# Earlier weight slabs, halved refills and unrolled pairs in the experts of a transformer block, one Trainium2 core

## The chip, the core and the metric

The kernel is one program on one core of a Trainium2 chip. It computes two transformer blocks for a sequence of 512 tokens, model width 1024, in float32. The metric is the device time of one execution in microseconds (us). Three runs of the kernel before gave 3689.02, 3692.55 and 3693.8 us; their median, 3692.55 us, is the time before.

## The reference, cut to what matters

The change touches the end of the mixer and the expert layer of the first block. Everything else (the mixer's branches, all of the second block) is left as it is.

```python
N_EXPERTS, EXPERT_FF, EC_CAPACITY = 16, 1024, 2        # D_MODEL 1024, SEQ 512

def ec_moe(h, router, w1, w3, w2):
    b_, n, _ = h.shape
    cap = EC_CAPACITY * n // N_EXPERTS                 # 64 tokens an expert
    aff = jax.nn.softmax(jnp.einsum('bld,de->ble', h, router).astype(F32), axis=-1)
    gate, idx = lax.top_k(jnp.swapaxes(aff, 1, 2), cap)
    bidx = jnp.arange(b_)[:, None, None]
    xe = h[bidx, idx]
    hid = jax.nn.silu(jnp.einsum('becd,edf->becf', xe, w1)) * jnp.einsum('becd,edf->becf', xe, w3)
    ye = jnp.einsum('becf,efd->becd', hid, w2) * gate[..., None].astype(h.dtype)
    return jnp.zeros_like(h).at[bidx, idx].add(ye)

# in first_block
x = x + g1 * rms_norm(ml, norm1_post[l])
h2 = rms_norm(x, norm2_pre[l]) * (1 + sc2) + sh2
x = x + g2 * rms_norm(ec_moe(h2, router[l], exp_w1[l], exp_w3[l], exp_w2[l]), norm2_post[l])
```

Each expert chooses its 64 tokens. The weights of the 16 experts are 16 x 3 x 4 MB = 201 MB, all of which must come from HBM.

## The kernel before, in words

The program is a chain of stages. A stage (function `stage`) is one block with a part for each engine; the parts meet only through semaphores, and between stages all engines meet at a barrier. Within a stage each engine runs its instructions in the order written. All large loads are issued by SyncE (SP), so their order is the order of SP's part.

Three stages lie around the change.

**settle** (the first of its three calls) multiplies the mixer's merged output `m` by `w_out`, adds it to `x`, normalises, stores `x` (L1760) and the normalised rows `xn_dram` (L1763) tile by tile, and computes the router's logits. SP first issues its loads (L1747 to L1757, the last one `se_hw`, the router's weights), then the stores of the four token tiles as VectorE finishes them. The normalised tile of a token tile t has one of two places in `se_xn`; for t = 2 and 3 VectorE waits until the store of tile t - 2 has landed (above L1924).

**choice_experts** routes and runs the experts. VectorE finds the 64 largest affinities of each expert in eight rounds (L2124 to L2127), and writes the token numbers to `chosen` (L2134). Then it builds `scat`, the matrices that will add the results back (L2137, eight instructions), and GpSimd gathers the 128 rows of the first pair of experts from `xn_dram` into `ex_xg` (L2043, an indirect DMA). TensorE transposes them (L2051, `turn`), VectorE scales them into `ex_xs` (L2144, `take_tokens`), and the products begin.

The experts are taken in eight pairs. The weights are cut into 96 slabs of 2 MB (128 partitions of 16 KB), in the order of use, 12 to a pair: eight for the products with w1 and w3 (`up`), four for w2 (`down`). One product (`both_experts`, L2060) takes two slabs, one for each expert of the pair, in 16 matmuls for each slab. After four products the hidden rows are transposed (L2072) and copied to `ex_hidT` (L2109), the next pair's rows are transposed (L2051), and the two down products follow; their results go to `ye` (L2161). The pairs are a loop on each engine (`Fori`), the last one outside it on TensorE and VectorE.

The slabs lie in `ex_ring`, six places, with a semaphore `slab_in` and a semaphore `slab_free` each. SP fills six places when the stage begins (L2024), and each further slab when both halves of its place's old slab have been used to the end (L2028):

```python
sp.wait_ge(slab_free[n % RING], i * 2 + (n // RING + 1))
sp.dma_start(ring[:, n % RING, :, :], w_slabs[bass.ds(i * PER + n, 1)].rearrange("a p k n -> p (a k) n")
             ).then_inc(slab_in[n % RING], 16)
```

**settle** (the second call) multiplies `scat` by `ye`, adds the result to `x` and goes on to the second block.

Of the kernel before, what the change touches and what calls it, by code (L numbers as in the profile page):

```python
# [20 lines left out]
P = 128  # L21
D = 1024
# [32 lines left out]
@contextmanager  # L55
def stage(nc):

    with ExitStack() as stack:
        s = Sems(nc, stack)
        with nc.Block() as block:  # L60
            yield s, block, stack
        nc.clear_and_free_semaphores(list(s.all.values()))
        nc.all_engine_barrier()  # L63
# [1649 lines left out]
def settle(nc, cst, source, rows, norm, x_in, x_out, cols, head, lg, xT=None, xn_dram=None, xn_keep=None):  # L1713
# [9 lines left out]
    with ExitStack() as keep:  # L1723
# [17 lines left out]
        with stage(nc) as (s, block, _):  # L1741
# [3 lines left out]
            def _(sp):  # L1745
# [240 lines left out]
CAP = 2 * SEQ // NE  # L1986


def choice_experts(nc, cst, lg, positions, idx, scat, xn_dram, a_col, sh_col, ring, w_slabs, ye):

    RING, PER = 6, 12
    NTT, PAIRS_E, ROUNDS = SEQ // P, NE // 2, CAP // 8
    ident, CT = cst("ident"), 6
    with ExitStack() as keep:
# [3 lines left out]
        affT = sb("ct_affT", [NE, 2, SEQ])  # L2001
# [7 lines left out]
        hidT = sb("ex_hidT", [P, KC, P])  # L2009
        ps = keep.enter_context(nc.psum_tensor("ex_ps", [P, 8, 512], F32, allow_name_mangling=True))  # L2010
        with stage(nc) as (s, block, _):
            slab_in = [s.named(f"slab_in{n}") for n in range(RING)]
            slab_free = [s.named(f"slab_free{n}") for n in range(RING)]
            halves = [slice(64 * j, 64 * j + 64) for j in range(2)]
            up = lambda h, m: 4 * h + 2 * m
            down = lambda h: 8 + 2 * h
            used = lambda i, n: i * 2 + (n // RING + 2)

            @block.sync
            def _(sp):  # L2020

                sp.dma_start(every[:, :], positions.broadcast_to([P, SEQ])).then_inc(s.every_in, 16)
                for n in range(RING):
                    sp.dma_start(ring[:, n, :, :], w_slabs[n]).then_inc(slab_in[n], 16)  # L2024

                def load(i, n):
                    sp.wait_ge(slab_free[n % RING], i * 2 + (n // RING + 1))
                    sp.dma_start(ring[:, n % RING, :, :], w_slabs[bass.ds(i * PER + n, 1)].rearrange("a p k n -> p (a k) n")  # L2028
                                 ).then_inc(slab_in[n % RING], 16)

                for n in range(RING, PER):
                    load(0, n)
                with sp.Fori(1, NE // 2) as i:
                    for n in range(PER):
                        load(i, n)

            @block.gpsimd
            def _(pool):
                pool.wait_ge(s.placed, 1)
                for g in range(NE // 2):  # L2040
# [5 lines left out]
            def _(pe):  # L2046
                def turn(i):

# [5 lines left out]
                def both_experts(i, n, src, bank):  # L2054

                    for j in range(2):
                        pe.wait_ge(slab_in[(n + j) % RING], i * 32 + 16 * ((n + j) // RING + 1))
                    for k in range(KC):
                        for j in range(2):
                            mm = pe.matmul(ps[halves[j], bank, :], src[:, k, halves[j]], ring[:, (n + j) % RING, k, :], start=k == 0, stop=k == KC - 1)  # L2060
                            if k == KC - 1:
                                mm.then_inc(slab_free[(n + j) % RING], 1)

                def pair(i, last):
                    pe.wait_ge(s.xs_ready, i + 1)
                    for h in range(2):
                        pe.wait_ge(s.hid_ready, i * 2 + (h + 1))
                        for m in range(2):
                            both_experts(i, up(h, m), xs, 2 * h + m)
                    pe.wait_ge(s.hid_ready, i * 2 + 4)  # L2070
                    for k in range(KC):
                        mm = pe.transpose(ps[:, 4 + k // 4, P * (k % 4):P * (k % 4) + P], hid[:, P * k:P * k + P], cst("ident"))  # L2072
                    mm.then_inc(s.hid_turned, 1)
                    pe.wait_ge(s.hidT_ready, i * 2 + 2)
                    if not last:
                        turn(i + 1)
                    for h in range(2):
                        pe.wait_ge(s.ye_kept, i * 2 + (h + 1))
                        both_experts(i, down(h), hidT, 6 + h)
# [9 lines left out]
                for n in range(RING):  # L2089
                    pe.sem_inc(slab_free[n], 1)  # L2090
                pe.sem_inc(s.hid_turned, 1)
                turn(0)
                with pe.Fori(0, NE // 2 - 1) as i:
                    pair(i, False)
                pair(NE // 2 - 1, True)

            @block.scalar
            def _(act):
                act.wait_ge(s.shifted, 1)
                act.activation(aff[:, :, :], aff[:, :, :], ACT.Exp).then_inc(s.exped, 1)  # L2100
                with act.Fori(0, NE // 2) as i:
                    act.wait_ge(s.hid_turned, i + 1)
                    for h in range(2):
                        n = up(h, 0) + 1
                        act.wait_ge(slab_free[n % RING], used(i, n))
                        act.activation(hid[:, 512 * h:512 * h + 512], ps[:, 2 * h, :], ACT.Silu).then_inc(s.silu, 1)  # L2106
                    act.wait_ge(s.hid_turned, i + 2)
# [4 lines left out]
            def _(dve):  # L2112
# [25 lines left out]
                dve.sem_inc(s.hid_ready, 2)  # L2138
                dve.sem_inc(s.ye_kept, 2)
# [8 lines left out]
                def pair(i, last):  # L2148
                    for h in range(2):
                        n = up(h, 1) + 1  # L2150
                        dve.wait_ge(s.silu, i * 2 + (h + 1))
                        dve.wait_ge(slab_free[n % RING], used(i, n))
                        part = hid[:, 512 * h:512 * h + 512]
                        dve.tensor_tensor(part, part, ps[:, 2 * h + 1, :], ALU.mult).then_inc(s.hid_ready, 1)  # L2154
                    if not last:
                        take_tokens(i + 1)
                    for h in range(2):
                        n = down(h) + 1
                        dve.wait_ge(slab_free[n % RING], used(i, n))
                        out = ye[:, bass.ds(i, 1), 512 * h:512 * h + 512].rearrange("p a n -> p (a n)")  # L2160
                        dve.tensor_copy(out, ps[:, 6 + h, :]).then_inc(s.ye_kept, 1)  # L2161

                take_tokens(0)
                with dve.Fori(0, NE // 2 - 1) as i:
                    pair(i, False)
                pair(NE // 2 - 1, True)


# [1059 lines left out]
def program(nc, a, out):  # L3228

    with ExitStack() as keep:  # L3230
# [14 lines left out]
        wide = lambda n: logits[:, 0:4 * n].rearrange("p (t n) -> p t n", t=4)  # L3245
        with ExitStack() as mixer:
# [14 lines left out]
            with ExitStack() as mg:  # L3261
# [63 lines left out]
```

## Time and profile before

| | |
|---|---|
| median of three runs | 3692.55 us |
| the profiled execution | 3690.78 us, its span 3689.0 us |
| TensorE busy | 3200.2 us, 87% of the span |
| VectorE, ScalarE, GpSimd busy | 40%, 27%, 1% |
| DMA over the whole span | mean 150 GB/s |
| DMA from about 2029 to 2398 us (4 of the 40 slices) | 428 GB/s in each |
| first settle stage | about 1889 to 1976 us |
| choice and experts | about 1976 to 2486 us |
| idle of TensorE before L2060, waiting for `ex_ring` | 63.1 us (of 66.1) in the up products, 10.9 us (of 12.9) in the down products |

The span is the time between the first and the last recorded instruction; the execution's own time is 1.8 us longer. Numbers of instructions on TensorE are counted twice, as matmuls (PE) and as weight loads (PEld), which run beside each other. A busy share says how much of a stretch an engine worked, not whether the next engine waited for it. For that the views of waits and of order in time are read.

### The profile page before, as it was taken

The page shows a single profiled execution, that of the slowest core. Times are in us where ns is not written, and L with a number is a line of the kernel's source. Part 1 is how long each engine was busy: PE and PEld are TensorE (multiplying, and loading weights), DVE is VectorE, ACT ScalarE, POOL GpSimd, SP SyncE. Part 2 cuts the span into 40 slices and gives each one's busy share as a digit, 9 for nine tenths or more (in the row PEclk, how much of TensorE's full clock was granted, in tenths as well). Part 3 has the DMA queues.
Part 4 walks back from the last instruction along what each step waited for, and adds up shares of the span by engine and source line. Part 5 has one row for each costly group of instructions (what it writes and reads, how often), then busy time and mean ns, then how long its engine had stood idle before and what let it go on. Part 6 is the DMA issues. An engine that isn't in the chain of part 4 may idle for free. (4 is left out here: it accounts for less than half of the span.)

```text
span 3689.0 us, 54736 instructions
## 1 busy us (share of the span) xinstructions
PE 3200.2 (87%) x23420; PEld 1783.0 (48%) x23420; DVE 1488.1 (40%) x3058; ACT 998.2 (27%) x1963; POOL 45.7 (1%) x65
## 2 busy tenths in 40 slices
PE   7889998889889999889995878777999999984996
PEld 3566666666765555544442323224454555541332
DVE  3666667666645676520014101003333324332122
ACT  2343443433213645620011000002233242320001
POOL 0000000000000000000000000000000000000000
PEclk9999999999879999889997999998999999986998
DMA  4112221122231222252024999982311111027998
GB/s 173 55 60 63 64 81 61 58 64 63 63 104 52 85 73 78 86 173 74 40 104 182 428 428 428 428 367 111 117 49 72 46 71 46 1 105 301 413 417 335
DMA packets 107203, 555.11 MB, mean 150 GB/s; under 512 B 30960, under 2 KB 33760, under 8 KB 82272
## 3 DMA queue, kind: packets, MB, share of 16 engines
q1 hardware_dynamic: 100832, 532.94, 37.4%
q0 software_dynamic: 3456, 12.58, 0.9%
q10 hardware_dynamic: 2688, 6.29, 0.4%
q8 instruction: 175, 2.87, 0.3%
q14 instruction: 52, 0.43, 0.0%
HBM read 518.03 MB, written 33.74 MB: 150 GB/s over the span
## 5 line engine op out<-in xcount | busy, mean ns | idle before, releaser
L2337 PE MATMUL mh_ps<-mh_w_ahead,xmT 128*128 128x512 f32 x768 | 336.3, 592 | 0.0
L2060 PE MATMUL ex_ps<-ex_ring,ex_xs 128*64 128x512 f32 x1024 | 243.7, 632 | 66.1 <-DMA ex_ring<-expert_slabs_in 63.1
L493 PE MATMUL rw_ps<-hT,rw_w 128*128 128x512 f32 (+1 forms) x640 | 258.9, 535 | 6.1 <-PEq L63 5.8
L2337 PEld LDWEIGHTS mh_ps<-mh_w_ahead,xmT 128*128 128x128 f32 x768 | 144.6, 190 | 167.0 <-issue 165.0
L2060 PEld LDWEIGHTS ex_ps<-ex_ring,ex_xs 128*64 128x64 f32 x1024 | 87.6, 145 | 221.7 <-issue 221.7
L1258 PE MATMUL sg_ps<-hTp,sg_w 128*128 128x512 f32 x384 | 170.3, 596 | 0.0
L493 PEld LDWEIGHTS rw_ps<-hT,rw_w 128*128 128x128 f32 x640 | 113.1, 192 | 89.6 <-issue 79.8
L2321 PE MATMUL mh_ps<-xmT,mh_w_ahead 128*128 128x512 f32 x256 | 127.0, 631 | 14.6 <-PEq L63 8.4
L2154 DVE TENSOR_TENSOR ex_hid<-ex_hid,ex_ps 128x512 f32<-128x512 f32 x16 | 11.0, 687 | 296.2 <-PE ex_ps L2060 296.2
L2060 PE MATMUL ex_ps<-ex_ring,ex_hidT 128*64 128x512 f32 x512 | 116.9, 610 | 12.9 <-DMA ex_ring<-expert_slabs_in 10.9
L1780 PE MATMUL se_ps<-se_w,se_mT 128*128 128x512 f32 x256 | 113.5, 600 | 7.6 <-DMA se_w<-w_out_in 7.6
L2964 PE MATMUL ge_ps<-ge_ring,ge_xs 128*64 128x512 f32 x512 | 116.1, 607 | 2.7 <-DVE ge_xsq L3059 2.7
L1258 PEld LDWEIGHTS sg_ps<-hTp,sg_w 128*128 128x128 f32 x384 | 73.8, 193 | 90.9 <-issue 90.8
L1482 DVE SCALAR_TENSOR_TENSOR sg_acc<-sg_ps,sg_par,sg_acc 128x510 f32<-128x510 f32 (+3 forms) x176 | 110.5, 628 | 6.2
L1297 PE MATMUL sg_ps<-sg_wz,hTp 128*128 128x512 f32 x256 | 112.2, 592 | 0.0
L1673 PE MATMUL mg_ps<-mg_pb,ybT 128*128 128x512 f32 x256 | 111.0, 592 | 0.0
L2106 ACT ACTIVATE ex_hid<-ex_ps 128x512 f32<-128x512 f32 x16 | 9.6, 597 | 361.5 <-PE ex_ps L2060 361.5
L1326 PEld LDWEIGHTS sg_ps<-sg_xdt,sg_kern 128*128 128x128 f32 x512 | 73.0, 211 | 46.3 <-issue 26.3
L1326 PE MATMUL sg_ps<-sg_xdt,sg_kern 128*128 128x64 f32 x512 | 72.9, 291 | 19.6 <-DVE sg_yacc L1545 10.4
L916 DVE TENSOR_TENSOR rw_xb<-rw_xb,rw_e 128x31 f32<-128x31 f32 (+15 forms) x248 | 85.2, 343 | 8.5
L1378 ACT ACTIVATE sg_kern<-sg_kern,tok 128x128 f32<-128x128 f32 x256 | 81.1, 390 | 26.5 <-DMA sg_kern<-cum_dram 26.5
L915 DVE TENSOR_TENSOR rw_e<-rw_low,rw_xb 128x31 f32<-128x31 f32 (+15 forms) x248 | 84.5, 341 | 6.9
(594 smaller groups left out, 5231.6 us busy)
## 6 DMA issues: line engine op xcount, KB each, us to landing
ex_ring<-expert_slabs_in SPq DMA_DIRECT2D x96, 2048.0 KB, 18.3
ge_ring<-expert_slabs_in SPq DMA_DIRECT2D x52, 2048.0 KB, 12.5
mh_w_ahead<-head_slabs_in SPq DMA_DIRECT2D x16, 2048.0 KB, 7.8
rw_mod_w<-mod_w_in SPq DMA_DIRECT2D x64, 384.0 KB, 4.1
rw_mod_w<-ada_in SPq DMA_DIRECT2D x64, 256.0 KB, 3.3
sg_kern<-cum_dram SPq DMA_DIRECT2D x64, 256.0 KB, 3.2
rw_w<-rw_slabs_in SPq DMA_DIRECT2D x8, 1536.0 KB, 7.0
sg_w<-xbc_blocks_in SPq DMA_DIRECT2D x24, 512.0 KB, 5.0
```

The costliest lines, as they stand in the source:

```text
L493: mm = pe.matmul(where[j, part], w[:, k, P * j:P * j + P], tokens, start=k == 0, stop=k == KC - 1)
L916: link(dve.tensor_tensor(xb[:, m:32, 0:m], xb[:, m:32, 0:m], part, ALU.subtract))
L1258: mm = pe.matmul(ps[:, A[j % 2], :], w[:, j, k, :], hTp[:, k, :], start=k == 0, stop=k == KC - 1)
L1297: mm = pe.matmul(ps[:, A[c % 2], :], hTp[:, k, P * c:P * c + P], wz[:, k, :], start=k == 0, stop=k == KC - 1)
L1326: mm = pe.matmul(ps[:, IN, v], kern[:, m % RING, P * h:P * h + P], xdt[:, m // 2 % 3, v], start=n % 4 == 0 and h == 0, stop=n % 4 == 3 and ...
L1482: link(dve.scalar_tensor_tensor(out[:, lo:hi], src[:, lo + i - 2:hi + i - 2], tap(i), out[:, lo:hi], ALU.mult, ALU.add))
L1673: mm = pe.matmul(ps[:, 4 * (n % 2) + j, :], src[:, k, off + P * t:off + P * t + P], w[:, k, :], start=k == 0, stop=k == nk - 1)
L1780: mm = pe.matmul(ps[:, ybank(t, h), :], left[:, k, tile(t)], right(k, h), start=k == 0, stop=k == KB - 1)
L2060: mm = pe.matmul(ps[halves[j], bank, :], src[:, k, halves[j]], ring[:, (n + j) % RING, k, :], start=k == 0, stop=k == KC - 1)
L2321: mm = pe.matmul(ps[:, 5 + b % 2, :], w[:, 0, k, P * b:P * b + P], xmT[:, k, :], start=k == 0, stop=k == KC - 1)
L2337: mm = pe.matmul(ps[:, 4 + t, :], xmT[:, k, P * t:P * t + P], w[:, slot, k, :], start=k == 0, stop=k == KC - 1)
L2964: mm = pe.matmul(ps[both[b], U[n], :], xs[:, i % 2, k, both[b]], up(2 * n + b)[:, k, :], start=k == 0, stop=k == KC - 1)
```

## The change

It has six parts.

1. Four slabs are loaded during the first settle stage, behind its own loads and ahead of its stores: slab 0 into a place of its own (`ex_first`), and slabs 8, 9 and 10 into `ye` and `scat`, which are not written until later.
2. The ring has eight places instead of six. With the three in `ye` and `scat`, which are used once, eleven slabs can lie in place. The choice stage begins with slabs 1 to 4; slabs 5 to 7 wait until the first gather has landed (`s.x_in`).
3. From slab 11 on a slab comes in two halves of 1 MB (four of the eight blocks k, 8 KB in each partition), each issued when the product that uses the place's old slab has got past that half. One semaphore `used`, raised twice by each product, replaces the `slab_free` semaphores.
4. The loops over the pairs are unrolled on all engines.
5. `scat` is built in the second pair, after `take_tokens`, instead of ahead of the first product.
6. `m` is allocated at the other end of the SBUF and freed after settle, `xmT` is allocated after the experts, and `affT` lies in `ex_hid`.

```diff
# settle, SyncE
                 sp.dma_start(hw[:, :, :], head_w).then_inc(s.head_in, 16)
+                for dst, src, landed in ahead:
+                    sp.dma_start(dst, src).then_inc(landed, 16)
                 for t in range(NTT):
# choice_experts
+EX_RING = 8
-    RING, PER = 6, 12
+    PER, REG, SPARE = 12, len(ring), len(spare)
+    FIRST = REG + SPARE
+            before = lambda g: g - REG if g >= FIRST + REG else g - FIRST
+            part_used = lambda g, part: 2 * (g // 2) + part + 1
# SyncE
                 sp.dma_start(every[:, :], positions.broadcast_to([P, SEQ])).then_inc(s.every_in, 16)
-                for n in range(RING):
-                    sp.dma_start(ring[:, n, :, :], w_slabs[n]).then_inc(slab_in[n], 16)
...
-                for n in range(RING, PER):
-                    load(0, n)
-                with sp.Fori(1, NE // 2) as i:
-                    for n in range(PER):
-                        load(i, n)
+                for g in range(1, 5):
+                    sp.dma_start(ring[g], w_slabs[g]).then_inc(slab_in[g], 16)
+                sp.wait_ge(s.x_in, 16)
+                for g in range(5, REG):
+                    sp.dma_start(ring[g], w_slabs[g]).then_inc(slab_in[g], 16)
+                for g in range(FIRST, TOTAL):
+                    dst, landed, _ = home(g)
+                    for half in range(2):
+                        ks = slice(4 * half, 4 * half + 4)
+                        sp.wait_ge(s.used, part_used(before(g), half))
+                        sp.dma_start(dst[:, ks, :], w_slabs[g][:, ks, :]).then_inc(landed, 16)
# TensorE
-                            if k == KC - 1:
-                                mm.then_inc(slab_free[(n + j) % RING], 1)
+                        if k % 4 == 3:
+                            mm.then_inc(s.used, 1)
...
-                with pe.Fori(0, NE // 2 - 1) as i:
-                    pair(i, False)
-                pair(NE // 2 - 1, True)
+                for i in range(PAIRS_E):
+                    pe.wait_ge(s.xs_ready, i + 1)
...
# VectorE
-                dve.wait_ge(s.every_in, 16)
-                for g in range(PAIRS_E):
-                    dve.tensor_scalar(scat[:, g, :], every[:, :], place[:, 0, g:g + 1], place[:, 1, g:g + 1], ALU.is_equal, ALU.mult)
...
                     if i + 1 < PAIRS_E:
                         take_tokens(i + 1)
+                    if i == 1:
+                        dve.wait_ge(s.every_in, 16)
+                        dve.wait_ge(s.used, down_used(0, 1))
+                        for g in range(PAIRS_E):
+                            dve.tensor_scalar(scat[:, g, :], every[:, :], place[:, 0, g:g + 1], place[:, 1, g:g + 1], ALU.is_equal, ALU.mult)
# program
+            spare = [as_slab(ye[:, 0:4, :]), as_slab(ye[:, 4:8, :]), scat[:, :, :]]
+                       ahead=[(first[:, :, :], a["expert_slabs"][0], early.named("slab_in0"))] +
+                             [(spare[n], a["expert_slabs"][EX_RING + n], early.named(f"spare_in{n}")) for n in range(len(spare))])
```

How the rows of three places stand, read from the built programs (no times in them). The first is SP in the first settle stage; before:

```order
L1753 DMA se_w<-w_out_in 128x4096
L1754 DMA se_g<-norm_pre_in 128x8
L1755 DMA se_sc<-mod 128x8x1
L1756 DMA col_sh<-mod 128x8x1
L1757 DMA se_hw<-router_in 128x128
L1760 DMA x<-se_x 128x1024
L1763 DMA xn_dram<-se_xn 128x1024
```

and now (the stores' lines have moved by two in the text):

```order
L1755 DMA se_sc<-mod 128x8x1
L1756 DMA col_sh<-mod 128x8x1
L1757 DMA se_hw<-router_in 128x128
L1759 DMA ex_first<-expert_slabs_in 128x4096
L1759 DMA ye<-expert_slabs_in 128x4096 x2
L1759 DMA scat<-expert_slabs_in 128x4096
L1762 DMA x<-se_x 128x1024
L1765 DMA xn_dram<-se_xn 128x1024
```

Four loads of 2 MB (4096 floats in each partition) stand between the router's weights and the first store.

The second is SP at the start of the choice stage. Before, with the first instructions of its loop:

```order
L2022 DMA ct_every<-positions_in 128x512
L2024 DMA ex_ring<-expert_slabs_in 128x4096 x6
L2028 DMA ex_ring<-expert_slabs_in 128x4096 x6
L2033 UNCONDITIONAL_BRANCH
L2033 ISA
L2028 ISA
L2028 DMA ex_ring<-expert_slabs_in 128x4096
```

and now:

```order
L2032 DMA ct_every<-positions_in 128x512
L2034 DMA ex_ring<-expert_slabs_in 128x4096 x4
L2037 DMA ex_ring<-expert_slabs_in 128x4096 x3
L2043 DMA ex_first<-expert_slabs_in 128x2048 x2
L2043 DMA ex_ring<-expert_slabs_in 128x2048 x14
L2043 DMA ex_first<-expert_slabs_in 128x2048 x2
```

Four slabs stand where six did, three more follow them, and all later loads are halves (2048 floats), 170 of them.

The third is VectorE from the choice of the tokens on. Before:

```order
L2134 CAST chosen<-ct_place 128x8
L2137 TENSOR_SCALAR scat<-ct_every,ct_place 128x512 x8
L2144 TENSOR_SCALAR ex_xs<-ex_ps,col_a,col_sh 128x128 x8
L2164 UNCONDITIONAL_BRANCH
L2164 ISA
L2152 REGISTER_ALU
L2154 TENSOR_TENSOR ex_hid<-ex_hid,ex_ps 128x512
```

and now:

```order
L2136 CAST chosen<-ct_place 128x8
L2141 TENSOR_SCALAR ex_xs<-ex_ps,col_a,col_sh 128x128 x8
L2151 TENSOR_TENSOR ex_hid<-ex_hid,ex_ps 128x512 x2
L2141 TENSOR_SCALAR ex_xs<-ex_ps,col_a,col_sh 128x128 x8
L2161 COPY ye<-ex_ps 128x512 x2
L2151 TENSOR_TENSOR ex_hid<-ex_hid,ex_ps 128x512 x2
L2141 TENSOR_SCALAR ex_xs<-ex_ps,col_a,col_sh 128x128 x8
L2158 TENSOR_SCALAR scat<-ct_every,ct_place 128x512 x8
L2161 COPY ye<-ex_ps 128x512 x2
```

The eight instructions that build `scat` have moved from ahead of the first pair to the middle of the second.

## Rows read from the trace of the kernel before

**Rows 1.** The profile page, costliest groups, the products of the experts:

```profile
L2060 PE MATMUL ex_ps<-ex_ring,ex_xs 128*64 128x512 f32 x1024 | 243.7, 632 | 66.1 <-DMA ex_ring<-expert_slabs_in 63.1
L2060 PE MATMUL ex_ps<-ex_ring,ex_hidT 128*64 128x512 f32 x512 | 116.9, 610 | 12.9 <-DMA ex_ring<-expert_slabs_in 10.9
```

**Rows 2.** Stretches: length, busy times (count), then granted clock, DMA share, GB/s:

```profile
1911.00:1932.00 21.00, 21.00 (x50) 9.31 (x49) 7.96 (x21) 6.81 (x18) 0.00 (x0) 1.00 0.14 54
1998.00:2009.00 11.00, 0.39 (x2) 0.28 (x2) 4.27 (x12) 1.28 (x1) 1.20 (x1) 0.50 1.00 424
2017.00:2025.00 8.00, 8.00 (x32) 2.71 (x30) 0.00 (x0) 0.00 (x0) 0.00 (x0) 0.75 0.00 1
2060.00:2460.00 400.00, 316.03 (x1380) 118.74 (x1378) 33.79 (x74) 22.50 (x32) 4.68 (x5) 0.95 1.01 428
```

**Rows 3.** TensorE in order of time, the first pair of experts and the last:

```profile
2011.05 1.97 PE L2051 MATMUL ex_ps<-consts,ex_xg 128*128 128x128 f32 x8 [12.49 <-DMA ex_xg<-xn_dram,chosen]
2016.04 30.10 PE L2060 MATMUL ex_ps<-ex_ring,ex_xs 128*64 128x512 f32 x128 [3.02 <-DVE ex_xs L2144]
2049.28 1.09 PE L2051 MATMUL ex_ps<-consts,ex_xg 128*128 128x128 f32 x8 [1.24 <-ACT ex_hidT L2109]
2050.29 7.09 PE L2060 MATMUL ex_ps<-ex_ring,ex_hidT 128*64 128x512 f32 x32
2109.24 1.59 PE L2051 MATMUL ex_ps<-consts,ex_xg 128*128 128x128 f32 x8 [1.24 <-ACT ex_hidT L2109]
...
2458.36 8.50 PE L2060 MATMUL ex_ps<-ex_ring,ex_xs 128*64 128x512 f32 x32 [2.70 <-DMA ex_ring<-expert_slabs_in]
2477.91 7.09 PE L2060 MATMUL ex_ps<-ex_ring,ex_hidT 128*64 128x512 f32 x32 [0.83 <-DVE ye L2161]
2486.66 34.57 PE L1780 MATMUL se_ps<-ye,scat 128*128 128x512 f32 x80 [1.66 <-PEq L63]
```

**Rows 4.** SP in order of time, 1970 to 2520 us (start, length, line, count):

```profile
1976.52 3.34 SPq L2024 DMA_DIRECT2D ex_ring<-expert_slabs_in  x6
2025.55 431.11 SPq L2028 DMA_DIRECT2D ex_ring<-expert_slabs_in  x90
```

**Rows 5.** GpSimd in order of time, the gathers of the first two pairs:

```profile
1999.47 1.20 POOL L2043 DMA_INDIRECT ex_xg<-xn_dram,chosen  x1 [965.96 <-DVE chosen L2134]
2013.29 0.94 POOL L2043 DMA_INDIRECT ex_xg<-xn_dram,chosen  x1 [12.63 <-PE ex_ps L2051]
```

**Rows 6.** The tile ex_xg, its gathers' time to landing, over the whole span:

```profile
DMA to landing us min/median/max: 4.3/10.8/11.5
```

**Rows 7.** VectorE in order of time, settle's third tile and the building of scat:

```profile
1948.60 0.76 DVE L1924 TENSOR_SCALAR se_xn<-se_x,se_rx 128x1024 f32<-128x1024 f32 x1
1999.09 3.73 DVE L2137 TENSOR_SCALAR scat<-ct_every,ct_place 128x512 f32<-128x512 f32 x8
```

**Rows 8.** DMA queues from 2060 to 2460 us (q0 is GpSimd's, q1 SP's):

```profile
q1 hardware_dynamic: 11568, 168.56, 99.0%
q0 software_dynamic: 743, 2.65, 1.6%
q8 instruction: 1, 0.02, 0.0%
```

**Rows 9.** SP in order of time in the first settle stage:

```profile
1908.36 2.84 SPq L1757 DMA_DIRECT2D se_hw<-router_in  x1
1928.40 0.32 SPq L1763 DMA_DIRECT2D xn_dram<-se_xn  x1
```

**Rows 10.** The page: the count of instructions, and the queue that fetches them:

```profile
span 3689.0 us, 54736 instructions
...
q8 instruction: 175, 2.87, 0.3%
```

**Rows 11.** DMA queues from 3370 to 3680 us, the second block's experts:

```profile
q1 hardware_dynamic: 8547, 106.58, 83.4%
q0 software_dynamic: 1152, 4.19, 3.8%
```

More of the change, by code:

```diff
@@ L55, in stage @@
 @contextmanager
-def stage(nc):
+def stage(nc, carried={}):
     with ExitStack() as stack:
@@ L1710, in _, with settle @@
                     dve.tensor_tensor(m[:, t, cols], ga_n, gb_n, ALU.add).then_inc(s.merged, 1)
-def settle(nc, cst, source, rows, norm, x_in, x_out, cols, head, lg, xT=None, xn_dram=None, xn_keep=None):
+def settle(nc, cst, source, rows, norm, x_in, x_out, cols, head, lg, xT=None, xn_dram=None, xn_keep=None, ahead=()):
     NTT, H, KB = SEQ // P, 2, 8
@@ L1986, with choice_experts @@
 CAP = 2 * SEQ // NE
-def choice_experts(nc, cst, lg, positions, idx, scat, xn_dram, a_col, sh_col, ring, w_slabs, ye):
-    RING, PER = 6, 12
+EX_RING = 8
+def choice_experts(nc, cst, lg, positions, idx, scat, xn_dram, a_col, sh_col, ring, spare, early, w_slabs, ye):
+    PER, REG, SPARE = 12, len(ring), len(spare)
+    FIRST = REG + SPARE
     NTT, PAIRS_E, ROUNDS = SEQ // P, NE // 2, CAP // 8
+    TOTAL = PER * PAIRS_E
     ident, CT = cst("ident"), 6
@@ L2009, in choice_experts, with home @@
         hidT = sb("ex_hidT", [P, KC, P])
+        affT = hid[0:NE, :].rearrange("e (n t) -> e n t", n=2)
         ps = keep.enter_context(nc.psum_tensor("ex_ps", [P, 8, 512], F32, allow_name_mangling=True))
-        with stage(nc) as (s, block, _):
-            slab_in = [s.named(f"slab_in{n}") for n in range(RING)]
-            slab_free = [s.named(f"slab_free{n}") for n in range(RING)]
+        with stage(nc, early.all) as (s, block, _):
+            slab_in = [early.named(f"slab_in{n}") for n in range(REG)]
+            spare_in = [early.named(f"spare_in{n}") for n in range(SPARE)]
             halves = [slice(64 * j, 64 * j + 64) for j in range(2)]
-            up = lambda h, m: 4 * h + 2 * m
-            down = lambda h: 8 + 2 * h
-            used = lambda i, n: i * 2 + (n // RING + 2)
+            before = lambda g: g - REG if g >= FIRST + REG else g - FIRST
+            part_used = lambda g, part: 2 * (g // 2) + part + 1
+            up_used = lambda i, h, m: part_used(PER * i + 4 * h + 2 * m, 1)
+            down_used = lambda i, h: part_used(PER * i + 8 + 2 * h, 1)
+            def home(g):
+                if g < REG:
+                    return ring[g], slab_in[g], 16
+                if g < FIRST:
+                    return spare[g - REG], spare_in[g - REG], 16
+                r = (g - FIRST) % REG
+                return ring[r], slab_in[r], 48 + 32 * ((g - FIRST) // REG)
             @block.sync
@@ L2052, in turn, with both_experts @@
                     mm.then_inc(s.x_turned, 1)
-                def both_experts(i, n, src, bank):
+                def both_experts(g, src, bank):
                     for j in range(2):
-                        pe.wait_ge(slab_in[(n + j) % RING], i * 32 + 16 * ((n + j) // RING + 1))
+                        _, landed, count = home(g + j)
+                        pe.wait_ge(landed, count)
                     for k in range(KC):
                         for j in range(2):
-                            mm = pe.matmul(ps[halves[j], bank, :], src[:, k, halves[j]], ring[:, (n + j) % RING, k, :], start=k == 0, stop=k == KC - 1)
-                            if k == KC - 1:
-                                mm.then_inc(slab_free[(n + j) % RING], 1)
[L2064 to L2079, printed above, removed]
+                            mm = pe.matmul(ps[halves[j], bank, :], src[:, k, halves[j]], home(g + j)[0][:, k, :], start=k == 0, stop=k == KC - 1)
+                        if k % 4 == 3:
+                            mm.then_inc(s.used, 1)
                 pe.wait_ge(s.affinity, 1)
@@ L2100, in _ @@
                 act.activation(aff[:, :, :], aff[:, :, :], ACT.Exp).then_inc(s.exped, 1)
-                with act.Fori(0, NE // 2) as i:
-                    act.wait_ge(s.hid_turned, i + 1)
[L2103 to L2107, printed above, removed]
+                for i in range(PAIRS_E):
+                    if i:
+                        act.wait_ge(s.hid_turned, i)
+                    for h in range(2):
+                        act.wait_ge(s.used, up_used(i, h, 0))
+                        act.activation(hid[:, 512 * h:512 * h + 512], ps[:, 2 * h, :], ACT.Silu).then_inc(s.silu, 1)
+                    act.wait_ge(s.hid_turned, i + 1)
                     for h in range(2):
```

74 lines of the change are left out of this document (39 added, 35 removed).

## Prediction, made before the changed kernel was run

> **What bounds the kernel now.** I read the page first. TensorE works 87% of the span, so as a whole the kernel is bound by TensorE; but the costliest groups show one place where it waits for something in bulk: before the products of L2060 it was idle 66.1 us, 63.1 of them for a DMA into `ex_ring`, and 12.9 us more before the down products, 10.9 for the same [rows 1]. The page's DMA row says why: 428 GB/s in four slices running. The stretches then show that this is flat: from 2060 to 2460 us the DMA share is 1.01 at 428 GB/s, while TensorE is busy 316 of 400 us [rows 2]. The order in time agrees: a pair of experts takes 2109.24 - 2049.28 = 59.96 us, and a pair's twelve slabs of 2.097 MB and one gather of 0.524 MB are 25.69 MB, at 428 GB/s 60.0 us [rows 2, 3]. So once the stream runs, its bytes alone set the pace, and nothing done for TensorE there is worth anything.
>
> What can be gained is time in which the stream does not run. The trace has two such stretches. The first is in settle: 54 GB/s from 1911 to 1932 us, where only its stores are left [rows 2]. The second is in the choice stage: SP issues six slabs from 1976.52 us, they are in by about 2009 us (424 GB/s until then), then nothing but the second gather, and 1 GB/s from 2017 to 2025, until SP issues the seventh slab at 2025.55, when the first product has used up slabs 0 and 1 [rows 2, 4]. From there 90 slabs follow without a hole to the end of the stage.
>
> **The new start of the stream.** From the order, slabs 5, 6 and 7 wait for the first gather, and everything behind them is on SP's queue after them. So the continuous stream starts when the gather has landed, and that time must be worked out. GpSimd issued it at 1999.47 us, and TensorE could start at 2011.05 [rows 3, 5]: 11.5 us to landing, the longest of the eight [rows 6]. It went out while the six slabs were still arriving at full rate [rows 2]. The second gather, issued at 2013.29 into an idle DMA, is the shortest, 4.3 us; the six within the stream take about 10.8 [rows 5, 6]. In the changed kernel only `ct_every` and slabs 1 to 4 are under way: 8.65 MB, at 428 GB/s 20.2 us, from about 1977.6 (6 slabs and `ct_every`, and the gather, took 31 us and ended about 2009), so they are in by 1998, before the gather is issued. I take 4.3 us plus the 0.26 us by which the first gather's own instruction is longer: the gathered rows are in place at 2004.0, 7.0 us earlier. `scat` is no longer ahead of `take_tokens`, but its 3.73 us from 1999.09 would end at 2002.8, before the gather lands, so moving it is worth nothing here [rows 7]. The first product then starts at 2016.04 - 7.0 = 2009.0 us, and slab 5 is issued at about 2004.1.
>
> **Does the stream run without holes from there?** Slabs 5, 6, 7 and the second gather are 6.82 MB, 15.9 us, so the first halved slab, 11, is wanted at about 2021. It goes where slab 0 was, and the first product's 32 matmuls, which began at the lower clock level of 1.2 GHz before (a mean of 0.75 of 2.4 GHz from 2017 to 2025 [rows 2]) and took from 2016.04 until slab 0's place was free at 2025.55, are done by 2009.0 + 9.5 = 2018.5. Slabs 11 to 18 take 39.2 us; 19 is wanted at 2060 and needs slab 11, used at about 2057.5 (2009.0, plus 30.1 for the up products, 4.15 from 2046.14 to 2050.29 for transposes and copies, and two down products of 7.09, so 48.4 [rows 3]). Slab 20 needs slab 12, whose product is half done at 2061, and is wanted at 2065. That is the tightest place, 3 to 4 us. After it TensorE's pair of 6 x 7.09 + 4.15 = 46.7 us is shorter than the stream's 60, so TensorE catches up in pair 2 or 3 and waits as before, with six places on order behind the two in use. I count no hole.
>
> **The sum.** Before: from 2025.55 [rows 4], 90 slabs and 6 gathers, 191.9 MB, 448.3 us at 428 GB/s, ending at 2473.8. After: from 2004.1, slabs 5 to 7 and 11 to 95 (88) and 7 gathers, 188.2 MB, 439.8 us, ending at 2443.9. That is 29.9 us earlier. The latencies at both ends are the same, and so is the tail: the product on slabs 90 and 91 starts at 2458.36, and 8.50 us for it, transposes, copies and two down products lead to 2485.0 [rows 3].
>
> **What the halves cost.** The trace has no stream of 1 MB loads, so this needs bounds. Per byte it has one pair of prices: from 2060 to 2460 us the gathers, whose pieces are rows of 4 KB, took 1.6% of the DMA engines for 2.65 MB, the slabs, in pieces of 16 KB, 99.0% for 168.56 MB: 0.604 against 0.587 per MB, 2.8% dearer [rows 8]. If that is a fixed cost of a piece, a piece of 8 KB lies 0.9% above one of 16 KB. 85 slabs come in halves, 416.5 us of stream: 4 us. The low bound is nothing (the 1.6 is rounded, the ratio may be 1.0); the high bound gives the halves the whole 2.8% of a piece half their size, 12 us. No row suggests a gain, since the share is 1.01 already. I take 4 us. SP's own 170 issues at 0.33 us are 56 us over a 440 us stage in which SP does nothing else.
>
> In this trace slabs follow one another at 4.90 us for 2.097 MB, at 428 GB/s and a share of 1.01: with others on the queue no slab pays a latency of its own [rows 2]. The Trainium skill speaks against the halves: DMA: Bandwidth & Descriptors, section Anatomy of one DMA, gives every DMA about 2 us beside its bytes, and its section Bandwidth has 341 GB/s for a transfer of 1 MB against 425 for 16 MB. If that ratio held within a stream, an estimate from the page would be 416.5 x (425/341 - 1) = 103 us more; that is a transfer by itself, and the trace does not agree for slabs. Whether it does for halves, no row shows; it stands with the third rival.
>
> **Other parts.** The four slabs in settle: SP issues them after `se_hw` (1908.36 plus 2.84 = 1911.2), 8.39 MB, 19.6 us, to about 1933. Behind them on the queue are the first tile's two stores, the later one issued at 1928.40; at 0.524 MB each they land by about 1937, and the first to wait for one is VectorE's L1924 of tile 2 at 1948.60, 11 us later [rows 7, 9]. So settle keeps its length; without that cover it would be pushed by up to the 19.6 us. Unrolling takes out loop branches under TensorE's waits, and adds instruction fetches, which in the loop were one packet in 400 us [rows 8]. The program's 54,736 instructions took 2.87 MB [rows 10], some 52 bytes each; the loop's body, 208 matmuls with their weight loads, is now there six more times: some 2,500 records of TensorE, 0.13 MB, 0.3 us of stream. A stall of TensorE is covered up to 13 us a pair. `scat` now stands behind `take_tokens` of the third pair, and the copy of `ye` behind it can only start when a down product of 7.09 us has ended; 3.73 us fit.
>
> Together -29.9 + 4 + 0.3, -25.6 us, all before the second settle, which runs as it did. Against its own execution: 3690.78 - 25.6 = 3665.2; that execution is 1.8 us under the median, so 3667 beside the median of the runs.
>
> **Rivals.**
> 1. The gather is not quicker. Its time may be something else than the six slabs (a first indirect DMA, say). Then the stream starts 7 us later: 3674. For it: the first is also the one with the longest instruction, 1.20 us. Against: six later ones, not first, show 10.8 within the stream, and one in an idle queue 4.3. 9%.
> 2. Settle pays. The stores or VectorE wait for the slabs' 19.6 us after all. That is taken from the gain: 3667 + 19.6 = 3686, near no change. Against: 11 us of room at the only wait. 4%.
> 3. The halves slow the stream, the rival on the slower side. In the second block's experts 4 KB rows cost 3.8% for 4.19 MB against 83.4% for 106.58 MB, 16% dearer per byte [rows 11]. At that price the 85 halved slabs take 416.5 x 0.16 = 67 us more, and the kernel stands at 3692.5 - 30 + 67 = 3730. It decides from 7.2% dearer on, where the 29.9 us are eaten. Against: those gathers run beside many other small transfers; within the slabs' own stream 4 KB rows are 2.8% dearer [rows 8]. 5%.
> 4. The stream has holes early on (slab 20, or TensorE's fetches at the first product), 5 to 15 us: about 3677. 8%.
> 5. No cost from the halves (3663), or a gain that I don't see, at the tail say: 3663 or below. 14%.
>
> **How the numbers follow.** 60% for the forecast, 3667, its own range 3662 to 3673. Rival 5 below reaches about 3656; rivals 1 and 4 above reach 3680. I give 3656 to 3681, leaving out rivals 2 and 3 and a little on either side. A measurement here tells 0.2%, 7.4 us, from no change. Faster by more: all but rivals 2, 3 and a remnant, 0.92; within it: most of rival 2, 0.04; slower: rival 3 less what stays small, 0.04.
>
> **What would show it.** The four loads on SP's queue at about 1911 and TensorE's products of settle unmoved; the first transpose at about 2004 and the first product at 2009; the DMA at over 420 GB/s from 2006 to about 2446 with no stretch near zero; 11 slabs' worth of products (to about 2057) and some pairs after it with no wait for `ex_ring`, then waits as before; the second settle starting at about 2461 instead of 2486.66 [rows 3]. If the rate of the halves is under 420, the 4 us were too few; under 400, rival 3. If the stage ends early by the sum but the kernel does not, something later takes it back, which I see no reason for.

## The result and the profile after

The changed kernel takes 3666.75 us, the median of five runs (3664.34 to 3674.42); the kernel before, 3690.36 us in five runs beside them. The ratio is 0.9941, 95% interval 0.9928 to 0.9954: faster by 0.46 to 0.72%. The forecast was 3667 us and the range 3656 to 3681. It was counted from 3692.55 us, the median of the first three runs before; with two more that median is 3690.36, so the gain in the medians is 23.6 us where 25.6 were forecast.

A median that meets the forecast to the microsecond proves little here, because runs of one kernel differ by 10 us (3664.34 to 3674.42 here). What the change does can be read more closely in a single trace, between two marks on SP's queue: the first load of the choice stage and the first load of the second settle. I call this the choice stage. First the two marks in the trace of before (start, length, engine, line), then those and the other issues of SP in the trace after:

```profile
1976.14 0.33 SPq L2022 DMA_DIRECT2D ct_every<-positions_in  x1
...
2486.61 0.33 SPq L1748 DMA_DIRECT2D se_gate<-mod  x1
```

```profile
1911.98 0.43 SPq L1759 DMA_DIRECT2D ex_first<-expert_slabs_in  x1
...
1929.31 0.33 SPq L1765 DMA_DIRECT2D xn_dram<-se_xn  x1
...
1977.05 0.33 SPq L2032 DMA_DIRECT2D ct_every<-positions_in  x1
1977.43 2.90 SPq L2034 DMA_DIRECT2D ex_ring<-expert_slabs_in  x4
2004.90 1.28 SPq L2037 DMA_DIRECT2D ex_ring<-expert_slabs_in  x3
2016.05 3.76 SPq L2043 DMA_DIRECT2D ex_first<-expert_slabs_in  x2
...
2465.50 0.33 SPq L1748 DMA_DIRECT2D se_gate<-mod  x1
```

The stage was 2486.61 - 1976.14 = 510.47 us long and is 2465.50 - 1977.05 = 488.45: 22.0 us less. The stage begins 0.91 us later than before, which comes from stages that the change does not touch; with that taken off, slabs 5 to 7 are issued at 2004.0, where [rows 4] have the stream's start at 2025.55.

GpSimd and TensorE after (start, length, and in brackets the idle time and its releaser):

```profile
2000.39 1.11 POOL L2051 DMA_INDIRECT ex_xg<-xn_dram,chosen  x1 [965.88 <-DVE chosen L2136]
```

```profile
2004.93 1.97 PE L2058 MATMUL ex_ps<-consts,ex_xg 128*128 128x128 f32 x8 [5.45 <-DMA ex_xg<-xn_dram,chosen]
2009.63 1.12 PE L2067 MATMUL ex_ps<-ex_first,ex_xs 128*64 128x512 f32 x1 [2.73 <-DVE ex_xs L2141]
...
2447.21 7.09 PE L2067 MATMUL ex_ps<-ex_ring,ex_hidT 128*64 128x512 f32 x32 [1.16 <-ACT ex_hidT L2111]
2456.80 7.09 PE L2067 MATMUL ex_ps<-ex_ring,ex_hidT 128*64 128x512 f32 x32 [2.51 <-DMA ex_ring<-expert_slabs_in]
2465.54 9.68 PE L1782 MATMUL se_ps<-ye,scat 128*128 128x512 f32 x22 [1.65 <-PEq L63]
```

From the gather's issue to the transposes it is 4.54 us, where [rows 3, 5] have 11.58. At the end the last product now waits 2.51 us for its slabs; in [rows 3] it waited for VectorE. The stretches after (length, busy times, clock, DMA share, GB/s):

```profile
1911.00:1932.00 21.00, 21.00 (x50) 9.29 (x49) 7.08 (x19) 6.55 (x17) 0.00 (x0) 1.00 0.94 377
2000.00:2002.00 2.00, 0.00 (x0) 0.00 (x0) 0.10 (x1) 0.00 (x0) 1.11 (x1) 0.50 0.00 0
2008.00:2017.00 9.00, 7.37 (x22) 2.29 (x24) 1.57 (x5) 0.00 (x0) 0.10 (x1) 0.60 1.00 426
2017.00:2025.00 8.00, 8.00 (x40) 2.67 (x38) 0.00 (x0) 0.60 (x1) 0.00 (x0) 1.00 0.99 419
2025.00:2100.00 75.00, 70.94 (x344) 25.26 (x340) 13.76 (x31) 3.94 (x7) 1.87 (x2) 1.00 1.01 421
2060.00:2420.00 360.00, 297.26 (x1288) 109.70 (x1286) 36.06 (x80) 14.20 (x25) 4.68 (x5) 0.93 1.01 421
```

The stretch from 2017 to 2025 us, which carried 1 GB/s in [rows 2], carries 419; settle's 54 GB/s has become 377 with TensorE as busy as before (x50); and the long stretch runs at 421 GB/s, not 428.

### The profile page after: what moved, and what is told of

Read it like the earlier page. It is cut to its first block and busy times, and to the rows that moved or that the text cites. A ratio compares the mean times of both kernels' runs of the same rounds, so it can differ in the third digit from the quotient of the medians.

```text
span 3664.9 us, 54483 instructions
## 1 busy us (share of the span) xinstructions
PE 3198.9 (87%) x23420; PEld 1778.7 (49%) x23420; DVE 1487.8 (41%) x3058; ACT 989.3 (27%) x1956; POOL 46.5 (1%) x65
## 5 line engine op out<-in xcount | busy, mean ns | idle before, releaser
L2067 PE MATMUL ex_ps<-ex_ring,ex_hidT 128*64 128x512 f32 x400 | 100.8, 606 | 7.6 <-DMA ex_ring<-expert_slabs_in 5.2
```

## The experiments

Each was profiled once, and its choice stage is measured between the marks above, in that one trace. "Timed" is the median of its runs, four to ten; the ratio is to runs of the kernel before taken beside them, whose medians were 3690.0 to 3691.6 us.

| kernel | choice stage, us | against | timed, us | ratio to before, 95% |
|---|---|---|---|---|
| before | 510.47 | | 3690.4 | |
| changed | 488.45 | -22.02 before | 3666.75 | 0.9928 to 0.9954 |
| e1_whole | 482.17 | -6.28 changed | 3663.69 | 0.9916 to 0.9944 |
| e4_pieces | 488.23 | -0.22 changed | 3666.2 | 0.9921 to 0.9953 |
| e2_no_gather_wait | 491.36 | +2.91 changed | 3668.87 | 0.9934 to 0.9966 |
| e3_late_slabs | 508.39 | +19.94 changed | 3691.02 | 0.9995 to 1.0014 |
| e7_unrolled_only | 512.48 | +2.01 before | 3692.22 | 0.9999 to 1.0018 |
| e6_gather_first | 505.24 | -7.24 e7 | 3686.72 | 0.9986 to 1.0005 |
| e5_ring6 | 497.25 | +8.80 changed | 3679.5 | 0.9966 to 0.9985 |
| e8_quarters | 502.51 | +14.06 changed | 3683.12 | 0.9971 to 0.9991 |
| f0_after (changed, again) | 488.45 | 0.00 changed | 3669.1 | 0.9929 to 0.9956 |
| f1_whole (e1, again) | 484.07 | -4.38 f0 | 3666.0 | 0.9911 to 0.9938 |

How far can a single trace be trusted? Two kernels were traced twice. The changed one repeats to a hundredth, the one with whole slabs only to 1.9 us, and that difference lies in the very last product, which takes 7.09 us at the full clock and more at a lower one. In e1_whole, f1_whole and e8_quarters, in this order:

```profile
2447.04 7.09 PE L2065 MATMUL ex_ps<-ex_ring,ex_hidT 128*64 128x512 f32 x32 [2.27 <-DMA ex_ring<-expert_slabs_in]
2449.14 8.78 PE L2065 MATMUL ex_ps<-ex_ring,ex_hidT 128*64 128x512 f32 x32 [2.68 <-DMA ex_ring<-expert_slabs_in]
2471.41 8.52 PE L2067 MATMUL ex_ps<-ex_ring,ex_hidT 128*64 128x512 f32 x32 [3.04 <-DMA ex_ring<-expert_slabs_in]
```

These two longer products are the only ones among the twelve traces. So the better measure of the stream is when the last product can start, counted from the stage's first mark: 479.75 us in the changed kernel and again in f0_after, 473.47 in e1_whole, 473.68 in f1_whole, 492.38 in e8_quarters.

The first settle stage, from its issue of `se_gate` to the mark of `ct_every`, was 86.2 to 86.4 us long in eleven of the twelve traces. In f0_after it was 87.74: there the granted clock was 0.51 from 1900 to 1906 us, before the four early slabs were issued at 1914, so they are not what made it longer.

**Whole slabs.** (The count that a product waits for changes with the number of loads to a slab; that line is left out here and below.)

```diff
-                    for half in range(2):
-                        ks = slice(4 * half, 4 * half + 4)
-                        sp.wait_ge(s.used, part_used(before(g), half))
-                        sp.dma_start(dst[:, ks, :], w_slabs[g][:, ks, :]).then_inc(landed, 16)
+                    sp.wait_ge(s.used, part_used(before(g), 1))
+                    sp.dma_start(dst, w_slabs[g]).then_inc(landed, 16)
```

> The changed kernel, but each slab from the 12th on comes in one load of 2 MB, issued when its place's old slab is used to the end. Stream theory (the end is the start of the stream plus its bytes over its rate, and halves cost rate): the rate returns from 421 to 428 GB/s, 178 MB of slabs come 7 us sooner, less a hole of 1 to 2 us where slabs 19 and 20 are wanted at once when their places come free; 3660 to 3662 us. Rival (the halves earn their keep by the earlier issue): holes of up to 3.5 us at several places, no gain, 3667 us or more. Rival (the 421 is not the halves' doing, but the eight places or the unrolled program's fetches): rate stays 421, 3667 us.

Measured: 482.17 us, and a rate of 427 to 429 GB/s from the start on. There is no hole where slabs 19 and 20 are wanted, at about 2056 and 2061 us:

```profile
2008.00:2060.00 52.00, 49.97 (x232) 17.14 (x230) 5.41 (x12) 2.27 (x4) 0.93 (x1) 0.96 1.01 429
2050.00:2100.00 50.00, 47.98 (x230) 16.85 (x228) 9.06 (x20) 2.27 (x4) 0.94 (x1) 1.00 1.01 428
2100.00:2400.00 300.00, 240.47 (x1048) 90.67 (x1046) 27.72 (x61) 11.34 (x20) 3.74 (x4) 0.94 1.01 427
```

The halves' earlier issue buys nothing here, and they cost the rate. Both rivals are out. The stage is 6.28 us shorter; the timed median, 3663.69 where 3660 to 3662 were expected, shows only 3 of them.

**Small pieces in whole loads.** The ring's seven places are laid out as two blocks, so that a slab there has two separate 8 KB pieces in a partition, but is one load. The eighth place, `ex_first`, stays whole. The lines cut to what matters:

```diff
-                ring = weights.enter_context(nc.sbuf_tensor("ex_ring", [P, EX_RING - 1, KC, 512], F32))
+                ring = weights.enter_context(nc.sbuf_tensor("ex_ring", [P, 2, EX_RING - 1, KC // 2, 512], F32))
+            shaped = lambda dst, src: src.rearrange("p (h k) n -> p h k n", h=2) if len(dst.shape) == 4 else src
...
+                    sp.wait_ge(s.used, part_used(before(g), 1))
+                    sp.dma_start(dst, shaped(dst, w_slabs[g])).then_inc(landed, 16)
```

> As e1_whole, but seven of the eight places lie in memory so that a slab of 2 MB consists of two pieces of 8 KB in each partition, 4 blocks k apart; it is still one load of 2 MB. It tells the size of a piece from the number of loads. If the 8 KB piece costs: the rate is 421 to 422 GB/s, about 3666 us. If the number of loads (one completion each) costs: 428 GB/s, 3660 us like e1_whole.

**Quarters.** Four loads of 0.5 MB to a slab, pieces of 4 KB:

```diff
-                    for half in range(2):
-                        ks = slice(4 * half, 4 * half + 4)
+                    for quarter in range(4):
+                        ks = slice(2 * quarter, 2 * quarter + 2)
-                        sp.wait_ge(s.used, part_used(before(g), half))
+                        sp.wait_ge(s.used, part_used(before(g), quarter // 2))
```

> The changed kernel with four loads of 0.5 MB for each slab from the 12th on, in pieces of 4 KB. Theory (a fixed cost for each piece, 10 ns on each DMA engine: 16 KB take 612 ns at 428 GB/s and 622 ns at 421): 642 ns, 408 GB/s, 14 us more than the changed kernel, 3680 us. Rival (what slowed is any splitting of a slab, once): 421 GB/s, 3667 us. Rival (SP's issuing, 340 loads, or the queue's length): more than 20 us.

From 2100 to 2400 us, e4_pieces and then e8_quarters:

```profile
2100.00:2400.00 300.00, 235.12 (x1043) 87.50 (x1041) 27.01 (x60) 11.34 (x20) 3.75 (x4) 0.95 1.01 422
```

```profile
2100.00:2400.00 300.00, 231.77 (x999) 85.48 (x994) 23.68 (x51) 11.34 (x20) 3.75 (x4) 0.94 1.03 409
```

With half as many loads as the changed kernel, e4_pieces has its rate (422 and 421) and its stage: it is the size of the piece, not the number of loads. A cost of the two-block layout itself, equal by chance to what fewer loads would have saved, would look the same; no run tells it apart. At 427, 421 and 409 GB/s over 16 engines, 16 KB take 614, 623 and 641 ns as one, two and four pieces: 9 ns for each piece more. For quarters no run keeps the number of loads apart from the piece; their price fits the same 9 ns.

Quarters came out 14.06 us longer in the stage where 14 were expected, but 1.4 of that is the last product at a lower clock. The last product starts 12.63 us later (492.38 - 479.75), and with whole slabs 6.1 to 6.3 earlier.

**The gather, from both sides.** Without SP's wait in the changed kernel, and with such a wait alone in the kernel before, whose loops are written out for it (a run of its own below):

```diff
# e2_no_gather_wait, from the changed kernel
-                sp.wait_ge(s.x_in, 16)
# e6_gather_first, from e7_unrolled_only
-                for n in range(RING):
+                for n in range(4):
+                    sp.dma_start(ring[:, n, :, :], w_slabs[n]).then_inc(slab_in[n], 16)
+                sp.wait_ge(s.x_in, 16)
+                for n in range(4, RING):
```

> The changed kernel without SP's wait for the first gather ahead of slabs 5 to 7. Theory: the gather takes 11 us again instead of 4.5 and the first product starts at about 2016 us, but slabs 5 to 7 are in by then; the stream goes on when the first product is half through, at about 2022 us, where it is at slab 11 at 2021 with the wait. So about 1 to 2 us slower, 3668 us. Rival (the gather's 7 us count in full): 3674 us. Rival (the wait is pure loss, the stream should start early): 3660 us.

> As e7_unrolled_only, and four of the first six slabs are issued at the start of the stage, the other two after the first gather has landed; ring of six, whole slabs, nothing loaded in settle, scat ahead of the first pair. It tests the gather alone. Theory: the gather lands 4.5 us after its issue instead of 11.5, the first product starts 7 us earlier, its places come free 7 us earlier, and so the stream of 90 slabs: choice stage 503.5 us, 3683 us. Rival (the first gather is slow of itself): 510 us, 3690 us. Rival (the two late slabs make TensorE wait): more than 510 us.

e6_gather_first, SP and GpSimd:

```profile
1975.42 0.33 SPq L2022 DMA_DIRECT2D ct_every<-positions_in  x1
1975.80 2.11 SPq L2024 DMA_DIRECT2D ex_ring<-expert_slabs_in  x4
2003.33 0.80 SPq L2027 DMA_DIRECT2D ex_ring<-expert_slabs_in  x2
2017.88 434.32 SPq L2031 DMA_DIRECT2D ex_ring<-expert_slabs_in  x90
```

```profile
1998.76 1.20 POOL L2046 DMA_INDIRECT ex_xg<-xn_dram,chosen  x1 [966.04 <-DVE chosen L2137]
```

SP goes on 4.6 us after the gather's issue (2003.33 - 1998.76), so it has landed by then though it is the first: rival 1 of the prediction is out. The stage is 7.24 us shorter than its neighbour without the order, e7_unrolled_only. It is 505.24 us where 503.5 were expected, since that neighbour already has 2 us more than the kernel before. Without the wait in the changed kernel the gather takes 11.80 us, from 1997.40 to this row:

```profile
2009.20 1.97 PE L2057 MATMUL ex_ps<-consts,ex_xg 128*128 128x128 f32 x8 [12.71 <-DMA ex_xg<-xn_dram,chosen]
```

The wait is worth less there, 2.91 us, since the late slabs fill the time until the first product has freed a place; without the wait that time is a hole. In e2_no_gather_wait again:

```profile
2012.00:2017.00 5.00, 3.10 (x8) 1.01 (x10) 1.85 (x6) 0.00 (x0) 0.38 (x1) 0.50 0.54 193
2017.00:2022.00 5.00, 5.00 (x20) 1.46 (x18) 0.00 (x0) 0.00 (x0) 0.00 (x0) 0.80 0.20 34
```

I had expected 1 to 2 us.

**Nothing loaded in settle.**

```diff
-                for dst, src, landed in ahead:
+                for dst, src, landed in ():
...
-                for g in range(1, 5):
+                for g in range(0, 4):
                     sp.dma_start(ring[g], w_slabs[g]).then_inc(slab_in[g], 16)
                 sp.wait_ge(s.x_in, 16)
-                for g in range(5, REG):
-                    sp.dma_start(ring[g], w_slabs[g]).then_inc(slab_in[g], 16)
+                for g in range(4, FIRST):
+                    dst, landed, _ = home(g)
+                    sp.dma_start(dst, w_slabs[g]).then_inc(landed, 16)
```

> The changed kernel without loads in the settle stage: slabs 0 to 3 at the start of the choice stage, slabs 4 to 10 after the first gather. Theory: four more slabs in the continuous stream, 4 x 4.9 = 19.6 us, so 3686 us. Rival (TensorE has 13 us of slack in each pair, so early slabs are worth little): 3667 to 3672 us.

The stage is 19.94 us longer, the four slabs at the stream's rate. Its first settle stage is 86.24 us without the early loads and 86.21 with them in the changed kernel, so they cost settle nothing. The timed median, 3691.02 where 3686 were expected, is 24 us over the changed kernel's, 4 more than the stage accounts for. Its ten runs go from 3685.07 to 3695.95, and the profiled one was the fastest; the four fastest show a mean granted clock of 0.936 to 0.939, the six others 0.933 to 0.936. Whether the clock is the whole of the 4 us stays open.

**A ring of six.**

```diff
-EX_RING = 8
+EX_RING = 6
```

> The changed kernel with six places in the ring instead of eight (with the three in ye and scat nine). The bytes after the gather are the same 88 slabs. Theory: the ring's size counts only until TensorE has caught up; the stream has a hole of 6 us before slab 9, whose place is free when the first product is half through, and one of about 4 us before slab 16, which waits for slab 10: 10 us more than the changed kernel, 3677 us, choice stage 498 us. Rival (two more places count for nothing, the early loads do it all): 3667 us. Rival (the ring must be eight deep in the steady part too): 3690 us or more.

8.80 us longer where 10 were expected (3679.5 us timed, for 3677). Both losses are in the trace: the first a hole from 2009 us, the second, from about 2049 to 2059, only a lower rate, with the full rate between and after:

```profile
2004.00:2009.00 5.00, 2.68 (x8) 0.83 (x10) 2.27 (x8) 0.00 (x0) 0.79 (x1) 0.50 0.95 401
2009.00:2014.00 5.00, 5.00 (x20) 1.59 (x18) 0.00 (x0) 0.00 (x0) 0.00 (x0) 0.72 0.23 61
2020.00:2045.00 25.00, 22.97 (x114) 8.41 (x112) 4.01 (x10) 1.67 (x3) 0.94 (x1) 1.00 1.01 422
2053.00:2058.00 5.00, 5.00 (x26) 1.66 (x24) 0.69 (x1) 0.00 (x0) 0.00 (x0) 1.00 0.89 300
2063.00:2100.00 37.00, 32.33 (x148) 12.24 (x146) 8.36 (x19) 1.67 (x3) 0.94 (x1) 0.95 1.01 422
```

TensorE is busy through both: it is the one that has not yet freed a place.

**Loops written out, nothing else.**

```diff
-                with pe.Fori(0, NE // 2 - 1) as i:
+                for i in range(NE // 2 - 1):
# and so on SyncE, ScalarE and VectorE
```

> The kernel before with its loops over the pairs written out on all engines, nothing else. Theory (the stream's bytes set the pace, branches lie under TensorE's waits): choice stage 510 us as before, 3690 us. Rival (the loops cost on the path, at the tail or per pair): 3 to 8 us less. Rival (fetching the written-out program costs): some us more.

2.01 us longer in one trace; by time alone it is not to be told from the kernel before, since the interval 0.9999 to 1.0018 contains 1. (So do those of e3 and e6.) But the loss is spread evenly over the stream. The hidden rows are transposed in the second pair and in the seventh, before and then e7_unrolled_only:

```profile
2106.91 1.09 PE L2072 MATMUL ex_ps<-consts,ex_hid 128*128 128x128 f32 x8 [0.79 <-DVE ex_hid L2154]
2407.03 1.09 PE L2072 MATMUL ex_ps<-consts,ex_hid 128*128 128x128 f32 x8 [0.79 <-DVE ex_hid L2154]
```

```profile
2109.58 1.09 PE L2072 MATMUL ex_ps<-consts,ex_hid 128*128 128x128 f32 x8 [0.86 <-DVE ex_hid L2154]
2411.16 1.09 PE L2072 MATMUL ex_ps<-consts,ex_hid 128*128 128x128 f32 x8 [0.86 <-DVE ex_hid L2154]
```

Five pairs take 300.12 us before and 301.58 here, 0.29 more for each; in e6_gather_first, written out too, they take 301.59. Its DMA queues from 2060 to 2360 us:

```profile
q1 hardware_dynamic: 8622, 125.62, 98.5%
q0 software_dynamic: 673, 2.43, 2.0%
q8 instruction: 8, 0.13, 0.2%
```

[Rows 8] have one packet of instructions in 400 us. The eight take 0.2% of the engines' time, which over the 450 us of stream is 0.9 us (the row is rounded to a tenth); the rate from 2100 to 2400 us is 427 where it was 428, 1 us more. That the fetches are all of the 2 us is not shown: what these rows account for is about 1 us.

**The changed kernel and whole slabs side by side.**

> The changed kernel again, to stand on the same chip beside f1_whole: choice stage 488.4 us, 3667 us.

> The kernel of e1_whole again (whole slabs): choice stage 482.2 us, 6.3 us less than f0_after, 3660 to 3664 us, if the stage's gain is not lost later. Rival (the later stages take it back, as the first pair of traces of the two could be read, 1199 us behind the stage against 1208): no more than 1 us apart.

f0_after repeats the stage of the changed kernel to a hundredth. f1_whole is 4.38 us shorter where 6.3 were expected, and 1.7 of the missing 1.9 is its last product at the lower clock; by that product's start it is 6.07 us earlier than f0_after, for 6.28 in the first pair. The timed medians differ by 3.1 us both times (3666.75 and 3663.69; 3669.1 and 3666.0), not the 6 of the stage and not the 1 or less of the rival, and the intervals overlap; where the other 3 go stays open. Whole slabs are the fastest version tried, by its stage clearly, by time alone not beyond doubt.

## Why the prediction was right, step by step

- **Bytes set the pace.** Right. Everything that the experiments changed and that was worth time moved the start of the stream, its bytes, its rate or a hole in it. Only the last product's 1.4 to 1.7 us at a lower clock, by chance of the run, came on top.
- **The stream starts at 2004.1.** Measured 2004.90, less the 0.91 us by which the stage began later: 2004.0. The gather took 4.54 us where 4.56 were counted. That it is slow beside the other loads is shown from both sides: 11.80 us in e2, where the loads are put back beside it, and 4.6 in e6, where they are taken away from the kernel before.
- **No hole.** Right: a share of 1.01 and 421 GB/s from 2025 to 2100 us and on. The counting behind it is borne out by the ring of six, whose two losses are where the same counting puts them (8.8 us for 10).
- **Settle keeps its length.** Right, 86.21 us after 86.33, and 86.24 in e3 without the early loads. The tile that was to wait first ran at 1949.50, 0.9 us later, as all did.
- **scat is free where it is.** Right. From the gather's issue to the first product it is 9.30 us in e6 (1998.76 to 2008.06), where `scat` is still built ahead, and 9.24 in the changed kernel (2000.39 to 2009.63), so moving it gained nothing, as counted; it had to move because slab 10 lies there. Its eight instructions run at 2092.41 for 3.73 us, and the copy of `ye` behind them still waits 0.73 us for TensorE:

```profile
2092.41 3.73 DVE L2158 TENSOR_SCALAR scat<-ct_every,ct_place 128x512 f32<-128x512 f32 x8
2096.88 0.69 DVE L2161 COPY ye<-ex_ps 128x512 f32<-128x512 f32 x1 [0.73 <-PE ex_ps L2067]
```

- **The halves cost 4 us.** The term was too small: they cost 6.3 in the stage. (The repetition's 4.4 is 6.1 when its slower last product is left out.) The working took the price from shares rounded to a tenth of a per cent ([rows 8]: 1.6% may be 1.55 or 1.65), which gave 0.9% for a piece of 8 KB; it is 1.5%. The bounds, 0 to 12 us, held it. The Trainium skill (DMA: Bandwidth & Descriptors, section Bandwidth) has 341 GB/s for 1 MB and 425 for 16 MB; an estimate from these would have been 103 us. Halves in a stream don't agree with it: 421 GB/s. The section's table is of transfers issued from GpSimd, and the slabs are SP's; no run here has a lone load of 1 MB.
- **Fetching the written-out loops costs 0.3 us.** Also too small: writing them out cost 2.0 by e7. The bytes were about right, 0.13 MB counted and 0.16 found over the whole program (2.87 MB in [rows 10], and now the row below, the same in e7), so it is not the bytes at the stream's rate that cost it. What does is open.

```profile
q8 instruction: 185, 3.03, 0.3%
```

- **The sum.** 25.6 us forecast, 22.0 found in the stage; of the 3.6 missing, 2.3 are the halves and 1.7 the written-out loops, which is 4.0; the 0.4 between them is about what single traces leave open. That the median still came out at 3667 is because the rest of the program fell well: the profiled execution is 24.1 us shorter, which is 22.0 in the stage, 3.0 behind it (3689.0 - 2486.6 = 1202.4 us before, 3664.9 - 2465.5 = 1199.4 after) and 0.9 lost ahead of it. The work behind the stage is the same in both, and the twelve traces range from 1199.4 to 1208.2 us there; the changed kernel alone has 1199.4 and, in f0_after, 1203.8. So the mechanism and the sign are right, the sum is 3.6 us too large, a seventh of it, and the exact hit is luck.

By parts, in the stage: the four slabs in settle give 19.9 us (e3), eight places instead of six 8.8 (e5), the order that lets the gather land early 7.2 alone (e6 against e7) but 2.9 in the changed kernel (e2); the loops take 2.0 and the halves 6.3. They don't add up to 22.0, since they partly fill the same hole, the one before the first product has freed a place: it opens in e2 (34 GB/s) and in e5 (61 GB/s). Without the early slabs the whole rest of the change is worth 2.1 us (510.47 - 508.39).

## What to carry to other kernels

Where a stream of loads runs flat, its end is its start plus bytes over rate: look for the times before it in which the DMA stands still, and for places in which early bytes can wait, and count for each place when it comes free against when the stream wants it. Keep what a critical small transfer must pass through free of large loads until it has landed, and give it the same loads afterwards. Don't split loads for an earlier issue unless a hole is there to fill; here the smaller pieces cost for as long as the stream ran. And when an effect is a few us and runs scatter by ten, measure between two marks around it, trace at least one kernel twice, and look what the last instruction did before you believe a difference of one or two.

## What the hardware showed that I had not expected

- Cutting 16 KB into two or four pieces costs 9 ns on the DMA engine for each piece more: 427, 421 and 409 GB/s. For pieces of 8 KB it does not matter whether they come in loads of 1 MB or of 2 MB (421 and 422).
- Writing out the loops lengthens the stage by 2.0 us of 510 (one trace each), 0.29 us in every pair, against 0.3 us in all that the instructions' bytes were counted to take at the stream's rate.
- ScalarE has less to do with the loops written out: from 2100 to 2400 us 25 records and 17.75 us before, 20 and 11.34 in e7_unrolled_only. What is gone is one table load of 1.28 us in each pair: eight in the stage before, one in e7. It was on no path here.
